# Half of the expert weight transfers issued by ScalarE's queue instead of SyncE's

## What is computed

```python
# top 4 of 32 experts for each token, softmax over the selected router logits
g = xblk @ w_gate[eid] + b_gate[eid]
u = xblk @ w_up[eid] + b_up[eid]
g = jnp.minimum(g, SWIGLU_LIMIT)
u = jnp.clip(u, -SWIGLU_LIMIT, SWIGLU_LIMIT)
hmid = (u + 1.0) * (g * jax.nn.sigmoid(SWIGLU_ALPHA * g))
y = hmid @ w_down[eid] + b_down[eid]
```

## Time and profile before

| | |
|---|---|
| median of 3 runs | 1379.7 us (1379.16 to 1381.84) |
| profiled execution: device time | 1377.93 us |
| its span | 1376.1 us |
| mean granted TensorE clock | 0.987 of full speed |
| TensorE busy | 1310.4 us (95%) |
| VectorE, ScalarE busy | 401.4 us (29%), 231.6 us (17%) |
| DMA | 468.64 MB, mean 341 GB/s; 82.2% of the engines' time for SyncE's queue |

### The profile page before, as it was taken

The page is one execution under the profiler, slowest core; times in us unless marked ns, Lnnn a source line. Parts: engine busy times, 40 slices in busy tenths (PEclk is TensorE's granted clock), DMA queues, the critical chain, the costliest instruction groups (busy, mean ns, idle before and its releaser), DMA issues.

```text
span 1376.1 us, 17863 instructions
## 1 busy us (share of the span) xinstructions
PE 1310.4 (95%) x6707; PEld 716.2 (52%) x6707; DVE 401.4 (29%) x1059; ACT 231.6 (17%) x423; POOL 37.2 (3%) x53
## 2 busy tenths in 40 slices
PE   7999899999899999999999999999999999999997
PEld 4887577888544434344343443435434344343466
DVE  2334532223442222322223222222322233222245
ACT  2221322202211111111011111112011110110123
POOL 1000411001000000000000000000000000000000
PEclk9999999999999999999999999999999999999999
DMA  8532265854399999999999999999999999999960
GB/s 282 170 123 92 70 222 183 307 214 187 124 422 414 420 422 422 422 422 421 423 422 421 422 423 421 422 422 422 422 422 422 422 422 422 422 422 421 422 233 32
DMA packets 102181, 468.64 MB, mean 341 GB/s; under 512 B 9806, under 2 KB 47996, under 8 KB 51460
## 3 DMA queue, kind: packets, MB, share of 16 engines
q1 hardware_dynamic: 96464, 456.33, 82.2%
q0 software_dynamic: 2544, 9.08, 1.9%
q10 hardware_dynamic: 3140, 2.79, 0.7%
HBM read 462.34 MB, written 5.83 MB: 340 GB/s over the span
## 4 chain that ended last, share of the span: by engine, by line
PE 89%; DVE 6%; DMA 3%; issue 2%; DVEq 0%; ACT 0%; SPq 0%; ACTq 0%
PE bank L747 49%; PE bank L563 17%; PE bank L762 8%; PE bank L782 4%; DVE hT L1263 2%; PE bank L755 2%; PE bank L851 2%; DMA ring<-in_w_up_dram 2%; PE bank L586 1%; PE bank L655 1%; DVE regC L1238 1%; PE bank L633 1%; PE bank L768 0%; PE bank L700 0%; DVE regC L1255 0%
## 5 line engine op out<-in xcount | busy, mean ns | idle before, releaser
L747 PE MATMUL bank<-ring,regC 128*64 128x512 f32 x3168 | 701.3, 598 | 10.7 <-DVE hT L1263 7.4
L747 PEld LDWEIGHTS bank<-ring,regC 128*64 128x64 f32 x3168 | 224.1, 138 | 434.8 <-issue 422.8
L1238 DVE TENSOR_TENSOR regC<-bank,biasT 128x512 f32<-128x512 f32 x66 | 45.3, 687 | 669.4 <-PE bank L755 669.4
L563 PE MATMUL bank<-regA,ring 128*128 128x264 f32 x896 | 210.1, 392 | 0.0
L563 PEld LDWEIGHTS bank<-regA,ring 128*128 128x128 f32 x896 | 168.5, 191 | 35.7 <-issue 7.2
L1263 DVE TENSOR_TENSOR hT<-hT,bank 128x264 f32<-128x264 f32 x272 | 98.1, 422 | 49.3 <-PE bank L782 49.3
L762 PE MATMUL bank<-regC,regB 128*128 128x128 f32 (+1 forms) x864 | 106.5, 283 | 0.0
L762 PEld LDWEIGHTS bank<-regC,regB 128*128 128x128 f32 x864 | 103.1, 196 | 5.9 <-issue 5.9
L1561 ACT ACTIVATE regD<-bank 128x512 f32<-128x512 f32 x66 | 39.4, 597 | 254.9 <-PE bank L747 254.9
L782 PE MATMUL bank<-regE,regD 64*128 64x264 f32 x544 | 78.7, 408 | 0.7 <-ACT regD L1570 0.7
L782 PEld LDWEIGHTS bank<-regE,regD 64*128 64x128 f32 x544 | 46.9, 186 | 36.3 <-issue 26.8
(11 more groups left out here) (269 smaller groups left out, 641.5 us busy)
## 6 DMA issues: line engine op xcount, KB each, us to landing
ring<-in_w_up_dram SPq DMA_DIRECT2D x132, 1024.0 KB, 21.8
ring<-in_w_down_dram SPq DMA_DIRECT2D x132, 1024.0 KB, 23.6
ring<-in_w_gate_dram SPq DMA_DIRECT2D x132, 1024.0 KB, 18.5
ring<-in_w_in_dram SPq DMA_DIRECT2D x28, 1024.0 KB, 5.4
out_dram<-ring POOLq DMA_DIRECT2D x9, 512.0 KB, 4.3
ring<-in_state_gla_dram POOLq DMA_DIRECT2D x8, 512.0 KB, 6.3
ring<-in_w_o_dram SPq DMA_DIRECT2D x4, 1024.0 KB, 8.1
ring<-in_w_ple_gate_dram SPq DMA_DIRECT2D x4, 1024.0 KB, 18.4
```

Source lines behind the costliest of these rows:

```text
L563: ins = mm(zbank((kind, f))[:, 0:T], by_col[s][:, k, half * P:(half + 1) * P], rhs[:, k, :], start=(k == 0), stop=(k == KT - 1))
L747: ins = mm(bank[b][n * CAP:(n + 1) * CAP, :], lhs(k + i), by_k[s][:, i, n * 512:(n + 1) * 512], start=(k + i == 0), stop=(k + i == KT - 1))
L1238: return v.tensor_tensor(out, v_in, bias.to_broadcast([P, HALF, 2, CAP]), ALU.add)
```

## The change

SyncE's loops over the refills take every second chunk number (step 2 from an even start). The odd ones are issued by ScalarE, in its own queue. ScalarE has no wait of its own for them: behind the copy of the gate rows it issues the refills of those of the slots of chunks 0 to 3 that hold odd numbers (chunks 1 and 3), behind the copy of the up rows those of chunks 5 and 7, and behind the copy of the down rows those of chunks 9 and 11. These copies have waited until the chunks concerned have been used. ScalarE's loop now runs seven rounds and the eighth is written out, since the last refills fall away. The short name of the change speaks of every second expert; the diff takes every second transfer.

```diff
-                for r in range(SLOTS, SLOTS + TURN):
+                for r in range(SLOTS, SLOTS + TURN, 2):
 
                     sp.wait_ge(chunk_used, i * TURN + (r - SLOTS + 1))
                     sp.dma_start(by_k[r % SLOTS], chunk_source(i * UNROLL + r // PER_EXPERT, r % PER_EXPERT))\
                         .then_inc(slot_loaded[r % SLOTS], 16)
-            for m in range(SLOTS + TURN * (ROUNDS - 1), LAST):
+            for m in range(SLOTS + TURN * (ROUNDS - 1), LAST, 2):
                 sp.wait_ge(chunk_used, m - SLOTS + 1)
                 load(m)
...
-            with act.Fori(0, ROUNDS) as i:
+
+            def refill(i, u, freed):
+
+                for c in freed:
+                    r = u * PER_EXPERT + c + SLOTS
+                    if r % 2 and (i is not None or r < UNROLL * PER_EXPERT):
+                        first = (ROUNDS - 1) * UNROLL if i is None else i * UNROLL
+                        act.dma_start(by_k[r % SLOTS], chunk_source(first + r // PER_EXPERT, r % PER_EXPERT))\
+                            .then_inc(slot_loaded[r % SLOTS], 16)
+
+            def main_round(i):
                 for u in range(UNROLL):
-                    j = i * UNROLL + u
+                    j = (ROUNDS - 1 if i is None else i) * UNROLL + u
                     rows_out(main, j, 4, 0, GATE_ROWS)
+                    refill(i, u, range(0, 4))
                     sigmoid(main, j)
                     rows_out(main, j, 8, 1, UP_ROWS)
+                    refill(i, u, range(4, 8))
                     gathered_out(main, j + 1, (u + 1) % 2, P if u % 2 else 0)
                     y_out(main, j)
+                    refill(i, u, range(8, 12))
+
+            with act.Fori(0, ROUNDS - 1) as i:
+                main_round(i)
+            main_round(None)
```

## The result

The changed kernel takes 1383.5 us (median of 18 runs, 1380.68 to 1384.99) against 1379.78 us for the kernel before, measured beside it (18 runs, 1377.08 to 1382.67). The ratio is 1.0024 with a 95% interval of 1.0017 to 1.0031: slower by 3.3 us, at least 2.3 and at most 4.3. The forecast was 1383.7 us, slower with a chance of 0.65.

The account below looks back on a forecast made before the run. DMA, full at 421 to 422 GB/s and slightly slower than TensorE, was taken as the bound in the expert stage. 0.9 us lost at the start and 3.3 of order gave +4.0 us, 1383.7 us forecast, range 1378.0 to 1391.

Parts of the forecast that it names:

- transfer 379 lands with no reserve: End of the main experts: the last up transfer lands at 1278.1 us, and any later landing is paid in full.
- SyncE's side and ScalarE's side, both 0: Expert stage: ending SyncE's held issues saves 0 under full DMA; ScalarE's issues cost 0, covered by its idle time.
- common limit of 11: Queues: one takes about 11 transfers; if two shared that limit, a pair on ScalarE could be held 10 us.
- Lost at the start, 0.9 us: Around 420 us: odd transfers go out late with almost no backlog, idling DMA 0.9 us net, bounds 0 and 3.
- The order, lead 1.3 and 3.3 us: Expert stage: SyncE's queue gets 1.3 transfers ahead and stays so; every odd transfer lands 3.3 us later.
- The sum: Transfer 379 at 1278.1 + 0.9 + 3.3 = 1282.3, plus 1.75 us of TensorE: 1284.1 instead of 1280.1, 4.0 us later.
- 4 us more in all, and no earlier: Last main expert: TensorE's waits for w_up grow by 4 us in all, with no such wait before it.
- Not slower through a better rate: DMA in the refills: two queues close gaps, 422 to 424 GB/s, 1378.3 us at best; 0.28 together with order absorbing it.
- slower through a worse one: DMA in the refills: two interleaved streams are served worse, one percent costing 9 us, 1393; chance 0.09.
- Not slower because the order hardly slips: Expert stage: lead under half a transfer, 1381.8 us; chance 0.28 together with the better rate.
- ScalarE held: Last 6 experts: ScalarE is held at a full queue, TensorE waits up to 5 us each, 1386 to 1398; chance 0.05.
- The sentence in the prediction from the Trainium skill: DMA: all issuers' transfers run on the same 16 engines and interleave; a second issuer saves only issue time, 0 here.

Follow-up runs that it names:

- e5: The change, with ScalarE issuing late in the first two rounds and at each chunk's release in the other six; ratio 1.0030 to the kernel before.
- e1: The change, with ScalarE waiting for each odd chunk's own release and issuing at once; ratio 1.0003 to the kernel before, 0.4 us slower.
- e3: The change, with ScalarE issuing all refills, four behind each of its three copies, and SyncE none; ratio 1.0099 to the kernel before, 13.7 us slower.
- e2: The change, with ScalarE issuing at each chunk's release in the first two rounds and late in the other six; ratio 0.9999 to the kernel before.

## Why the prediction was right, step by step

- **The bound and the place.** The step "transfer 379 lands with no reserve" holds: in both profiles of the kernel before TensorE waits for it, and in the kernels with two queues of equal share the delay of its landing is paid one for one to the end of the last weight chunk (3.89 us in the change, 3.77 in e5, 2.04 in e1). The time need not show it to the last microsecond: behind the stage the clock gives or takes 1.7 us.
- **SyncE's side and ScalarE's side, both 0.** They hold. SyncE's held issues are gone and nothing came of it. At 1160 us all 16 slots of the change have a transfer issued and not landed, eight of each queue, and no issue is held up; the one queue of the kernel before holds up its issuer with at most 12 of them issued. So the two queues have no common limit of 11, and ScalarE never met one. e3, which fills one queue from ScalarE, shows what would have happened: waits for ScalarE.
- **Lost at the start, 0.9 us.** It measured 1.2 us (both profiles of the change) against the first profile of before and 0.8 against the second, so 0.9 lies inside what can be told. The place was right too: a loss in the expert before, at 379 us, and the loss of the kernel before at 418 us smaller.
- **The order, lead 1.3 and 3.3 us.** The lead measured 1.1 to 1.2, that is 2.7 to 3.0 us. It moved between 0.8 and 2.2 until transfer 56 and stayed at 1.09 to 1.12 (1.19 to 1.23 in the second profile) from transfer 60 on, 120 us behind the start of the stage. That it is set early and stays is shown by e2 and e5 from both sides.
- **The sum.** 0.9 + 3.3 = 4.2 forecast for the landing, 3.89 and 4.21 measured (0.4 less against the second profile of before); 4.0 forecast for the time from the profile, 3.3 (2.3 to 4.3) by the ratio, 3.98 by the first profile. The step from 4.2 to 4.0 has a slip: it lets TensorE work 1.75 us on transfer 379, where the earlier trace rows have 1.94 and 0.04 until it starts. The work is the same before and after, so 4.2 at the landing should have given 4.2 in the time.
- **What was wrong: "4 us more in all, and no earlier".** TensorE waits from 1106 us on, in every second expert at the end of up. The step that failed looked at the reserve of the last pair only. Transfer 307 in the profile of before had 3.17 us in hand, and 3.88 us of lateness use that up six experts before the last. Of the 3.89 us TensorE has lost 0.8 when it starts on transfer 307, 2.7 at 331 and 3.2 at 355, so only 0.7 us are left for the last pair. The sum is not changed by it, because DMA does not pause in this part of the stage: a wait that comes early is one that need not come late.
- **Rivals.** Not slower through a better rate, and slower through a worse one: both fall with 422 GB/s from 446 us on in both kernels. Not slower because the order hardly slips (a lead under half a transfer): it falls with a lead of 1.1. ScalarE held: it falls for the change and is real in e3. The sentence in the prediction from the Trainium skill (DMA: Bandwidth & Descriptors, Issuing engines are not separate DMA queues) holds in this trace, with 50.8% and 50.4% for the two queues and no more bytes per second than one moved; by it alone the time would not have changed, and 3.3 us more were measured. The other one, of the ceiling of 435 GB/s, which the same page states, found nothing here: the long stretch, from 446 us to 1250, has 422 in both kernels.

## What to carry to other kernels

Where one queue already keeps the DMA engines full, as here, a second one adds no rate; it replaces the order of need by an order of two halves, and a transfer of the slower half is late by the lead that the other gained while both were nearly empty. So if work is shared between two queues, issue both parts at the moment of release at least at the start, and look at the landings of each queue apart, at the point where the reserve is smallest. A late issue behind a deep backlog cost nothing that could be measured (e2, at most 1.1 us). And when a span is compared to a microsecond, look at the granted clock of the parts that the change does not touch.

## What the runs showed of the hardware that was not expected

- The lead is conserved: between transfers 97 and 379 of the change, some 700 us, the lateness of the odd ones stays between 3.85 and 4.07 us.
- Near the start of the stage the engines ran at 205 to 328 GB/s for 2.4 us with three to four transfers of two queues issued and not landed (e1), and at 287 to 369 at the same place in e2, so issuing at once did not bring back all of the time at the start.
- Two queues held 16 transfers of 1 MB between them, eight each, without stopping their issuers, where one queue stopped its issuer with at most 12 issued. How many one of two queues would hold was not tried, since each can have only eight slots.
- The same 32 matmuls behind the stage took 9.04 us in seven profiles and 7.36 in three, and the granted clock is the one difference that the traces show.
